# Second block's attention scores: three products of split operands in place of one plain fp32 product

## The reference

```
q_l, k_l, v_l = _attn_heads(pl[4], pl[5], pl[6], q_norm_g[l], k_norm_g[l], rope)
q_c, k_c, v_c = _attn_heads(pc[4], pc[5], pc[6], q_norm_g[l], k_norm_g[l], None)
keys = jnp.concatenate([k_l, k_c], axis=1)
att_l = _sdpa_blocks(q_l, keys, vals)
if not last:
    att_c = _sdpa_blocks(q_c, k_c, v_c)
```

## Time and profile before

| what | value |
|---|---|
| median of 3 runs | 2245.72 us (2245.28 to 2247.11) |
| the profiled execution | 2245.23 us |
| its span, first to last instruction | 2243.4 us |
| instructions | 33841 |
| chain that ended last, by engine | PE 83%, DVE 8%, ACT 3% |
| granted TensorE clock, mean | 0.993 |
| attention loop of the second block, layer 0 | about 1165 to 1254 us |
| the same, layer 1 | about 1957 to 2016 us |

### The profile page before, as it was taken

How to read it: one execution, slowest core, us unless ns; L and a number is a source line. 1 busy time by engine, 2 the same in 40 slices (tenths; PEclk the granted TensorE clock), 3 DMA queues, 4 the chain that set the end, 5 groups by cost and what they waited for, 6 DMA issues and landing times.

```text
span 2243.4 us, 33841 instructions
## 1 busy us (share of the span) xinstructions
PE 2188.3 (98%) x13238; PEld 1935.3 (86%) x13238; DVE 1483.2 (66%) x2767; ACT 966.4 (43%) x1599; POOL 34.2 (2%) x37
## 2 busy tenths in 40 slices
PE   8899999999999999999999999999999999999998
PEld 6789987778997999988888888888889999979997
DVE  6869888779888567655446543643565766666666
ACT  5564445474545454432225422213245444344342
POOL 0000000000000010000000000000000100000000
PEclk9899999999999999999999999999999999999999
DMA  5457775547775411212331233333313225425653
GB/s 194 133 158 244 235 233 161 191 158 231 244 245 181 125 39 39 56 51 92 94 85 30 74 109 99 94 86 110 115 58 104 57 70 161 128 58 171 181 177 119
DMA packets 194725, 291.02 MB, mean 130 GB/s; under 512 B 9892, under 2 KB 86980, under 8 KB 194312
## 3 DMA queue, kind: packets, MB, share of 16 engines
q1 hardware_dynamic: 192320, 283.10, 40.7%
q10 hardware_dynamic: 2248, 5.77, 0.8%
HBM read 287.77 MB, written 1.06 MB: 129 GB/s over the span
## 4 chain that ended last, share of the span: by engine, by line
PE 83%; DVE 8%; ACT 3%; DVEq 2%; issue 2%; DMA 1%; ACTq 0%; SPq 0%
PE bank L2019 23%; PE bank L2021 22%; PE bank L2020 22%; DVE WLO L1008 2%; PE bank L2476 2%; PE bank L2694 1%; PE bank L2718 1%; PE bank L2415 1%; PE bank L2416 1%; PE bank L2498 1%; ACT WHI L516 1%; DMA RAW<-in_e_w_in 1%; PE bank L2421 1%; PE bank L2511 1%; PE bank L2219 1%
## 5 line engine op out<-in xcount | busy, mean ns | idle before, releaser
L516 ACT ACTIVATE WHI<-RAW 128x1024 fp32r<-128x1024 f32 (+2 forms) x500 | 506.1, 1016 | 838.3 <-PE bank L2021 807.8
L1008 DVE TENSOR_TENSOR WLO<-RAW,WHI 128x1024 fp32r<-128x1024 f32 (+2 forms) x500 | 581.2, 1170 | 426.8 <-ACT WHI L516 416.8
L2019 PE MATMUL bank<-ATH,WHI 128*128 128x256 f32 (+1 forms) x2032 | 664.7, 327 | 9.3 <-DVE h L1063 1.7
L2021 PE MATMUL bank<-ATH,WLO 128*128 128x256 f32 (+1 forms) x2032 | 652.0, 321 | 0.0
L2020 PE MATMUL bank<-ATL,WHI 128*128 128x256 f32 (+1 forms) x2032 | 651.9, 321 | 0.0
L2019 PEld LDWEIGHTS bank<-ATH,WHI 128*128 128x128 f32 x2032 | 386.8, 190 | 43.9 <-DVE WLO L1008 3.8
L2020 PEld LDWEIGHTS bank<-ATL,WHI 128*128 128x128 f32 x2032 | 387.1, 190 | 28.5 <-issue 0.7
L2021 PEld LDWEIGHTS bank<-ATH,WLO 128*128 128x128 f32 x2032 | 386.9, 190 | 28.3
L2019 PE MATMUL bank<-WHI,ATH 128*128 128x512 f32 (+2 forms) x996 | 357.2, 359 | 11.6 <-DVE ARENA L1053 5.1
L2020 PE MATMUL bank<-WLO,ATH 128*128 128x512 f32 (+2 forms) x996 | 352.4, 354 | 0.0
L2021 PE MATMUL bank<-WHI,ATL 128*128 128x512 f32 (+2 forms) x996 | 352.4, 354 | 0.0
(11 more groups left out here) (295 smaller groups left out, 2339.1 us busy)
## 6 DMA issues: line engine op xcount, KB each, us to landing
RAW<-in_w_in SPq DMA_DIRECT2D x192, 512.0 KB, 3.7
RAW<-in_w_ff SPq DMA_DIRECT2D x128, 512.0 KB, 4.5
ARENA<-in_w_ada SPq DMA_DIRECT2D x64, 384.0 KB, 4.6
RAW<-in_o_w_in SPq DMA_DIRECT2D x24, 512.0 KB, 4.1
RAW<-in_e_w_in SPq DMA_DIRECT2D x16, 512.0 KB, 4.8
RAW<-in_w_ple_gate SPq DMA_DIRECT2D x16, 512.0 KB, 3.9
RAW<-in_w_br_gla SPq DMA_DIRECT2D x16, 512.0 KB, 3.5
RAW<-in_w_br_attn SPq DMA_DIRECT2D x16, 512.0 KB, 3.5
```

Source lines behind the costliest of these rows:

```text
L516: nc.scalar.activation(WHI[:, slot, 0:n], RAW[:, slot, 0:n], ACT.Copy).then_inc(hi_split, 1)
L1008: V.tensor_tensor(WLO[:, slot, 0:n], RAW[:, slot, 0:n], WHI[:, slot, 0:n], ALU.subtract).then_inc(lo_split, 1)
L2019: mm(o, ah, bh, start=start, stop=False, skip_group_check=free)
L2021: return mm(o, al, bh, start=False, stop=stop, skip_group_check=free)
```

## The change

K2H, K2L, QSH and QSL are views of BTH and BTL: two key heads, and two queries. `keys_done` also splits K2 into K2H and K2L. `rotate` also splits the rotated query into QSH and QSL, and a_q is signalled after that. `scores` calls `product` on the four split operands in place of the plain `mm`.

```
+        K2H, K2L = BTH[:, 0:AKV, :], BTL[:, 0:AKV, :]
+        QSH, QSL = BTH[:, AKV:AKV + 2, :], BTL[:, AKV:AKV + 2, :]
...
-                    V.tensor_tensor(QS[:, r, 0:S], QS[:, r, 0:S], ROTW[:, r, :], ALU.add).then_inc(a_q, 1)
+                    V.tensor_tensor(QS[:, r, 0:S], QS[:, r, 0:S], ROTW[:, r, :], ALU.add)
+                    drain()
+                    V.tensor_copy(QSH[:, r, 0:tq], QS[:, r, 0:tq])
+                    drain()
+                    V.tensor_tensor(QSL[:, r, 0:tq], QS[:, r, 0:tq], QSH[:, r, 0:tq], ALU.subtract).then_inc(a_q, 1)
...
                     for kv in range(AKV):
                         V.tensor_tensor(K2[:, kv, :], KG[:, kv, :], bank[6 + kv][:, :], ALU.mult)
+                    drain()
+                    V.tensor_copy(K2H, K2)
+                    drain()
+                    V.tensor_tensor(K2L, K2, K2H, ALU.subtract)
...
                     for t in range(nq):
-                        q = QS[:, r, t * P:(t + 1) * P]
+                        q = [a[:, r, t * P:(t + 1) * P] for a in (QSH, QSL)]
                         if t < NT:
-                            last = mm(bank[3 * r + t][:, :], q, K2[:, kv, :], start=True, stop=True)
+                            last = product(bank[3 * r + t][:, :], *q, K2H[:, kv, :], K2L[:, kv, :], True, True)
                         else:
-                            last = mm(bank[3 * r + 2][:, (t - NT) * S:(t - NT + 1) * S], q, K2[:, kv, S:TOK], start=True, stop=True)
+                            last = product(bank[3 * r + 2][:, (t - NT) * S:(t - NT + 1) * S], *q, K2H[:, kv, S:TOK], K2L[:, kv, S:TOK], True, True)
```

## The result

The changed kernel has a median of 2247.68 us over 20 runs (2244.16 to 2250.87), the kernel before 2244.67 us over 20 (2238.99 to 2247.46). The ratio is 1.0014, with a 95% interval of 1.0008 to 1.0021: slower by 3.1 us, 1.8 to 4.7. The forecast was 2247.1 us and +1.9.

What follows compares the result with a forecast made beforehand. PE, busy 98% of the span, was taken as the bound, in layer 1 in a closed chain with DVE. Layer 0's -1.1 us and layer 1's +3.0 gave +1.9 on 2245.2: 2247.1 us, range 2242.5 to 2250.8.

Steps and rivals of the forecast that it cites:

- PE's part: Scores on PE: 2.58 to 2.09 us in layer 0, 1.72 to 1.37 in layer 1; 6.7 us less over all heads.
- DVE's part: Rotate on DVE: a CAST, a subtraction and drains add 1.25 us in layer 0, 0.85 in layer 1.
- The slack of 0.71 in layer 0: PE's wait for a_q before values, layer 0: 0.71 us spare, so 0.54 of the 1.25 us split becomes waiting.
- The term that was too small: Layer 0, heads 2 to 6: scores 0.49 us shorter, 0.54 us of new waiting, so +0.05 each.
- Cover: Keys' split in keys_done, about 2.06 us on DVE: counted as nothing; without cover in layer 1, 1.3 us once.
- head 0 of layer 1 would lose about 0.4 us: Layer 1: a_q(1) comes 0.65 us late, so scores(1) starts at 1962.72 in place of 1962.32, +0.40.
- The 0.2 us of the shorter `scores(0)`: Layer 1, head 0: of the 0.35 us that scores ends sooner, 0.2 was let reach maxima.
- Hidden split: Rival: values does not wait for the split, so all of PE's 6.7 us show, 2238.5 us; chance 0.08.
- Costly change of type: Rival: going from plain fp32 to fp32r at scores costs 14 x 0.19 = 2.7 us, 2249.8 us; chance 0.08.
- the sign that the prediction named for it: PE's first matmul of scores standing 0.4 us from the second would show a cost of going to fp32r.
- Slack used up by DVE's other work in layer 0: Rival: stored, gain and divide delay maxima or rotate in layer 0, 3.6 us more, 2250.7 us; chance 0.13.
- Lower clock: Rival: PE's clock falls because PE idles about 1.0 us of each 7.1 us pass in layer 1, 2255 us; chance 0.04.

Runs made afterwards that it cites:

- e2: The changed kernel without the split in rotate; scores are three fp32r products reading the keys' split operands in place of the query's. Ratio 0.9970 to the kernel before.
- e1: The changed kernel with scores left as plain fp32 products, so only the splits are added. Ratio 1.0038 to the kernel before.
- e6: The kernel before with only the keys' split in keys_done added. Ratio 0.9996 to the kernel before, within noise.
- e7: The kernel before with the whole change made in layer 0 alone. Ratio 0.9996 to the kernel before, within noise.
- e8: The kernel before with the whole change made in layer 1 alone. Ratio 1.0013 to the kernel before, 2.9 us slower.
- e3: The changed kernel with values waiting only until DVE has read bank 6, not for a_q. Ratio 0.9968 to the kernel before.
- e4: The kernel before with values waiting only until DVE has read bank 6, not for a_q. Ratio 0.9980 to the kernel before.
- e5: The changed kernel with the query's subtraction and a drain repeated before a_q. Ratio 1.0053 to the kernel before.

## Why the prediction was right

**Direction and range.** +1.9 was forecast, 3.1 (1.8 to 4.7) measured, 2247.68 in the range and 0.6 from the forecast. Inside the loops, with head 0's share: layer 0 gives 0.0 - 0.5 = -0.5 us (forecast -1.1), layer 1 gives 60.0 - 56.5 - 0.25 = +3.3, or +2.9 with before's own loop of 56.8 (forecast +3.0). The sum is +2.4 to +2.7. The closeness of the time itself is in part luck: the forecast was added to an execution of 2245.2, 0.5 above the median of the 20 runs, and the medians then differed by 3.0, 1.1 more than forecast. The first error took off about half of the second.

**PE's part.** Forecast from starts and not from durations: 2.09 us for layer 0's scores, 2.10 measured; passes without the split 9.17 and 6.28 reckoned, 9.17 and 6.30 measured (e2). The Trainium skill's formula (TensorE: Matmul & The Clock Gate, Back-to-back issue gap), which the section gives for one matmul in isolation, leads to an estimate of 1.95 for layer 0's scores; this trace does not agree, and the measured 2.10 decides.

**DVE's part.** 1.25 and 0.85 us forecast, 1.26 and 0.86 in the timeline and 0.87 in e1's passes. The CAST of 256 columns, which before did not show, took 0.294; 0.29 had been put between 0.15 and 0.42.

**Slack.** The slack of 0.71 in layer 0 was real: the new gap is 1189.39 - (1188.64 + 0.23) = 0.52, forecast 0.54. In layer 1 there was none, as said.

**The term that was too small.** Layer 0's pass was forecast to grow by 0.05 and grew by 0.15. `values` to the true start of `scores` takes 1192.06 - 1189.39 = 2.67 us after a wait; it took 2.59 without one, since its first matmul needs about 0.07 more behind a stall (from L2728 to L2731 1.80 us in the pass shown; 1.73 in layer 0 of before). Layer 1 paid that before already. Six waits, of `values(0)` to `values(5)`, at about 0.1 each are the 0.6 that separate -0.5 from -1.1.

**Cover.** The keys' split cost nothing (e6). That head 0 of layer 1 would lose about 0.4 us by `scores(1)` starting later was right as well: from `scores(0)` it starts 1959.15 - 1953.80 = 5.35 us later, before 1962.32 - 1957.26 = 5.06, and its first matmul takes 0.33 to the second where an unstalled one takes 0.23. The 0.2 us of the shorter `scores(0)` that the prediction let through to `maxima` measured 0.25.

**Rivals.** Hidden split: e1 shows all of it in layer 1, and in layer 0 what exceeds the slack. Costly change of type: the sign that the prediction named for it is there, since the record of the first matmul of `scores` stands 0.42 from that of the second (1191.87 and 1192.29). It was a bad sign, for the record starts early; the passes of e2 (9.17 and 6.30) leave no room for such a cost. Slack used up by DVE's other work in layer 0: that did not happen, since the gap is 0.52 and without the slack would be 1.25. Lower clock: the two loops of the kernel after, as stretches (busy us of each engine, clock, DMA share, GB/s), have a granted clock of 1.00, with PE busy for 54 of 61 us in the second.

```profile
1162.00:1250.00 88.00, 85.47 (x447) 72.42 (x446) 59.33 (x142) 45.24 (x103) 0.00 (x0) 1.00 0.18 50
1954.00:2015.00 61.00, 53.76 (x333) 47.54 (x332) 45.15 (x112) 31.03 (x63) 0.00 (x0) 1.00 0.29 78
```

## What to carry to other kernels

A cheaper instruction on the busiest engine is worth its saving only where the operands it needs cost less, on the chain of that stage, than it saves: here 1.25 and 0.85 us of splitting stood against 0.49 and 0.35 of product, and only slack made layer 0 come out even. Before a wait is lengthened, ask what each waiter needs: `values` needed only the read of a bank, not the sum, and a semaphore signalled there turned +0.14% into -0.32%; in the kernel before, without the new products, it gave about 2.5 us by itself. Read the two passes of a loop in starts, not in durations, and not in the idle time in brackets either, which hides the tail of the matmul before.

## What had not been expected of the hardware

The first 110 us differ from one execution to the next by as much as the whole effect, with the granted clock. Stretches of before and then of after (busy us of each engine, clock, DMA share, GB/s):

```profile
90.00:100.00 10.00, 9.36 (x46) 7.78 (x42) 8.03 (x39) 6.34 (x23) 0.00 (x0) 0.50 0.21 67
100.00:110.00 10.00, 10.00 (x66) 9.06 (x66) 8.34 (x41) 7.13 (x26) 0.00 (x0) 0.74 0.16 53
```

```profile
90.00:100.00 10.00, 8.71 (x59) 7.75 (x60) 9.11 (x46) 7.84 (x30) 0.00 (x0) 0.83 0.22 73
100.00:110.00 10.00, 10.00 (x81) 9.13 (x80) 9.78 (x49) 9.25 (x35) 0.00 (x0) 1.00 0.35 107
```

In before PE ran at 1.2 GHz through all of 90 to 100 us (0.50); in after only part of that stretch did. Both kernels do the same work there, and after started `scores(0)` of layer 0 at 1162.16, 3.4 us sooner than before (1165.54), which is why its profiled span is the shorter one. It is not the only such stretch. In the profiles of e1 to e7 the clock also fell near 450 us, where before, after and e8 had 1.00; the row of e3:

```profile
450.00:460.00 10.00, 10.00 (x52) 9.16 (x53) 3.66 (x21) 6.29 (x22) 0.00 (x0) 0.55 0.28 80
```

Over the 20 runs of the kernel after, the fastest (2244.16) had a mean clock of 0.996 and the slowest (2250.87) 0.990, and over all 20 the correlation of time and clock is -0.85. The fit described under e4, made for each experiment with its own runs of before, gives +10.0 us for e1, -7.1 for e2, -7.8 for e3, +12.3 for e5, -0.2 for e6, -0.5 for e7 and +2.8 for e8. Each is within its interval (0.8 to 1.3 us either way) of what the loops give. For the runs of before that the kernel after was compared with, no clocks are on record, so its 3.1 us can't be corrected in this way. The clock goes with most of the spread of about 7 us; what makes it fall in one run and not in another is not shown.
